# Chunk products ordered by shape, and the inverse's second form made by transposes that ScalarE copies

## The reference, cut to what matters

```python
proj = rmsnorm(x, g_mix) @ w_in            # columns: RWKV | MLA | gates
# RWKV-7, for each of 16 heads of 64, token by token:
sa = S @ kk_t
S  = S * w_t[None, :] + outer(v_t, k_t) - outer(sa, kk_t * a_t)
y_t = S @ r_t
# then group norm, bonus, gate; y_a = y @ w_o_a
# MLA: latent attention over past and new latents; y_b = o @ w_o_b
h = x + (sigmoid(Ga) * y_a + sigmoid(Gb) * y_b) @ w_out
h = h + (silu(causal_conv(gate)) * up) @ w_ffn_down   # gate, up = rmsnorm(h) @ w_ffn_in
y = rmsnorm(h, g_final)
```

## Time and profile before

| | us |
|---|---|
| median of 3 timed runs | 2621.8 (2618.93 to 2631.11) |
| profiled execution | 2617.77 |
| its span, first to last instruction | 2616.1 |
| TensorE busy | 2551.1 (98%) |
| TensorE weight loads busy | 2353.6 (90%) |
| VectorE busy | 1201.2 (46%) |
| ScalarE busy | 848.4 (32%) |
| TensorE's share of the chain that ended last | 95% |
| mean granted TensorE clock | 0.995 |

### The profile page before, as it was taken

The page is one execution under the profiler, slowest core; times in us unless marked ns, Lnnn a source line. Parts: engine busy times, 40 slices in busy tenths (PEclk is TensorE's granted clock), DMA queues, the critical chain, the costliest instruction groups (busy, mean ns, idle before and its releaser), DMA issues.

```text
span 2616.1 us, 40662 instructions
## 1 busy us (share of the span) xinstructions
PE 2551.1 (98%) x15484; PEld 2353.6 (90%) x15484; DVE 1201.2 (46%) x1855; ACT 848.4 (32%) x1247; POOL 108.4 (4%) x182
## 2 busy tenths in 40 slices
PE   6999999999999999999999899999999999999997
PEld 6888888888888999999987799999878999999886
DVE  4566566665644333334433444444333444444233
ACT  4332233322223333334422433333222333333232
POOL 3000000000001010000000000000000000000010
PEclk9999999999999999999999999999999999999999
DMA  5321222212244343334453344444333444444443
GB/s 171 90 63 43 55 68 69 67 40 60 61 104 123 104 121 101 102 90 129 127 168 121 96 128 127 123 127 128 121 121 130 127 125 124 128 128 126 143 126 129
DMA packets 414494, 283.46 MB, mean 108 GB/s; under 512 B 31729, under 2 KB 392691, under 8 KB 413409
## 3 DMA queue, kind: packets, MB, share of 16 engines
q1 hardware_dynamic: 405600, 259.16, 33.7%
q0 software_dynamic: 8832, 23.43, 3.1%
HBM read 275.62 MB, written 6.92 MB: 108 GB/s over the span
## 4 chain that ended last, share of the span: by engine, by line
PE 95%; DVE 3%; ACT 1%; issue 1%; DMA 1%; POOL 0%; DVEq 0%; SPq 0%; POOLq 0%; ACTq 0%
PE banks L1392 19%; PE banks L836 17%; PE banks L838 17%; PE banks L837 17%; PE banks L315 2%; PE banks L418 2%; PE banks L429 2%; PE banks L433 2%; PE banks L847 2%; PE banks L848 2%; PE banks L849 2%; PE banks L484 1%; PE banks L483 1%; PE banks L1255 1%; PE banks L508 1%
## 5 line engine op out<-in xcount | busy, mean ns | idle before, releaser
L826 DVE TENSOR_TENSOR w_lo<-w_raw,w_hi 128x1024 fp32r<-128x1024 f32 x482 | 590.2, 1225 | 978.2 <-ACT w_hi L821 976.5
L836 PE MATMUL banks<-x_hi,w_hi 128*128 128x384 f32 x2640 | 910.0, 345 | 7.4 <-DVE w_lo L826 7.4
L838 PE MATMUL banks<-x_hi,w_lo 128*128 128x384 f32 x2640 | 883.4, 335 | 0.0
L837 PE MATMUL banks<-x_lo,w_hi 128*128 128x384 f32 x2640 | 882.9, 334 | 0.0
L821 ACT ACTIVATE w_hi<-w_raw 128x1024 fp32r<-128x1024 f32 x482 | 511.2, 1061 | 1041.2 <-PE banks L838 605.1
L836 PEld LDWEIGHTS banks<-x_hi,w_hi 128*128 128x128 f32 x2640 | 496.0, 188 | 22.6 <-DVE w_lo L826 9.3
L837 PEld LDWEIGHTS banks<-x_lo,w_hi 128*128 128x128 f32 x2640 | 496.3, 188 | 4.8
L838 PEld LDWEIGHTS banks<-x_hi,w_lo 128*128 128x128 f32 x2640 | 495.6, 188 | 0.0
L1392 PE MATMUL banks<-w_hi,act_hi 128*128 128x512 f32 x528 | 164.0, 392 | 4.7 <-DVE h_rows L1951 2.4
L1392 PE MATMUL banks<-w_hi,act_lo 128*128 128x512 f32 x528 | 163.9, 392 | 0.0
L1392 PE MATMUL banks<-w_lo,act_hi 128*128 128x512 f32 x528 | 163.7, 391 | 0.0
(11 more groups left out here) (390 smaller groups left out, 2606.5 us busy)
## 6 DMA issues: line engine op xcount, KB each, us to landing
w_raw<-in_w_ffn_in SPq DMA_DIRECT2D x176, 512.0 KB, 4.0
w_raw<-in_w_in SPq DMA_DIRECT2D x144, 512.0 KB, 3.8
w_raw<-in_w_ffn_down SPq DMA_DIRECT2D x88, 512.0 KB, 3.6
w_raw<-in_w_out SPq DMA_DIRECT2D x32, 512.0 KB, 3.6
w_raw<-in_w_o_a SPq DMA_DIRECT2D x16, 512.0 KB, 3.9
w_raw<-in_w_o_b SPq DMA_DIRECT2D x16, 512.0 KB, 3.9
w_raw<-in_w_in SPq DMA_DIRECT2D x20, 256.0 KB, 3.7
w_ukv_head<-in_w_ukv POOLq DMA_DIRECT2D x8, 512.0 KB, 4.2
```

Of the source, the lines that this page charges most:

```text
L826: nc.vector.tensor_tensor(lo[:, s], raw[:, s], hi[:, s].bitcast(F32), ALU.subtract).then_inc(lo_done, 1)
L836: nc.tensor.matmul(out, hi[:, s, k, :], xh[:, kt, :], start=kt == 0, stop=False)
L837: nc.tensor.matmul(out, hi[:, s, k, :], xl[:, kt, :], start=False, stop=False)
L838: last = nc.tensor.matmul(out, lo[:, s, k, :], xh[:, kt, :], start=False, stop=kt == 15)
```

## The change

1. On levels 0 to 3 the product for `t_y` (line 433) and VectorE's subtraction (726) are gone. Instead, levels 1 to 4 begin with TensorE's transposes of the `t_x` that the level before has updated, and ScalarE copies them into `t_y`. Level 4 keeps its update of `t_y`.
2. Levels 0 to 3 get a second piece, behind the update product; the end of the round has four pieces instead of eight.
3. The cuts move: on ScalarE cut 2 comes between the copies of levels 2 and 3, cut 3 behind the last copy, cut 4 in the chunk steps, cut 5 ahead of the state rows; VectorE's follow.
4. In the chunk steps the outputs come first, both heads of each kind together, with both products from u and then the signal for y; then the gain's products from v, and then those from u. VectorE no longer waits for y.

The semaphores `t_x_ps` and `t_x_done` become `form_ps` and `form_done`, which count five times a round.

```diff
             for lv in range(5):
                 if lv == 0:
-                    pe.wait_ge(E("t_x_done"), f + 1)
+                    pe.wait_ge(E("form_done"), f * 5 + 1)
                 else:
-                    pe.wait_ge(E("t_done"), f * 9 + (2 * lv - 1))
+                    pe.wait_ge(E("t_done"), f * 5 + lv)
+                    for i, t in units(lv - 1):
+                        last = transpose(head_tile(2, i, t), t_x[:, 3 * i + t, :])
+                    last.then_inc(E("form_ps"), 1)
                 for i, t in units(lv):
                     u = 3 * i + t
                     last = mm_(head_tile(g_bank(lv), i, t), n_t[:, u, :], t_x[:, u, :], start=True, stop=True)
                 if lv == 0:
                     pe.wait_ge(E("mt_done"), f + 1)
                 else:
-                    pe.wait_ge(E("t_done"), f * 9 + 2 * lv)
+                    pe.wait_ge(E("form_done"), f * 5 + (lv + 1))
                 if lv < 4:
                     for i, t in units(lv):
                         u = 3 * i + t
                         last = mm_(head_tile(10 - g_bank(lv), i, t), t_y[:, u, :], t_g[:, u, :], start=True, stop=True)
-                    last.then_inc(E("dt_ps"), 1)
-                for i, t in units(lv):
-                    u = 3 * i + t
-                    last = mm_(head_tile(2, i, t), t_g[:, u, :], t_y[:, u, :], start=True, stop=True)
+                else:
+                    for i, t in units(lv):
+                        u = 3 * i + t
+                        last = mm_(head_tile(2, i, t), t_g[:, u, :], t_y[:, u, :], start=True, stop=True)
                 last.then_inc(E("dt_ps"), 1)
+                if lv < 4:
+                    pieces(1)
 
...
                 gain = [ps[heads(i), 4, 0:64] for i in range(2)]
                 yo = [ps[heads(i), 5, cols] for i in range(2)]
                 for i in range(2):
-                    mm_(gain[i], tok[r0:r0 + 64, 0, t, heads(i)], v[r0:r0 + 64, t, heads(i)], start=True, stop=False)
                     mm_(yo[i], v[:, t, heads(i)], c_k[:, 3 * i + t, cs], start=True, stop=False)
-                    if c:
+                if c:
+                    for i in range(2):
                         mm_(yo[i], st[:, 1, :], rh[:, i, cols], start=False, stop=False)
                 pe.wait_ge(E("u_done"), f * 4 + (c + 1))
-                mm_(yo[0], un[:, 0, heads(0)], c_b[:, t, cs], start=False, stop=True)
+                for i in range(2):
+                    last = mm_(yo[i], un[:, 0, heads(i)], c_b[:, 3 * i + t, cs], start=False, stop=True)
+                last.then_inc(E("y_ps"), 1)
+                for i in range(2):
+                    mm_(gain[i], tok[r0:r0 + 64, 0, t, heads(i)], v[r0:r0 + 64, t, heads(i)], start=True, stop=False)
                 for i in range(2):
                     last = mm_(gain[i], tok[r0:r0 + 64, 1, t, heads(i)], un[r0:r0 + 64, 0, heads(i)],
                                start=False, stop=True)
                 last.then_inc(E("state_ps"), 1)
-                mm_(yo[1], un[:, 0, heads(1)], c_b[:, 3 + t, cs], start=False, stop=True).then_inc(E("y_ps"), 1)
...
             pieces(4)
             if more:
                 pe_s0(f + 1)
-            pieces(8)
+            pieces(4)
...
             if more:
                 nc.scalar.preload_act_table_set("sigmoid_and_others")
             act.wait_ge(E("bonus_done"), f + 1)
-            cut(2)
+            for lv in range(1, 5):
+                n = NT if lv < 4 else 2 * P
+                act.wait_ge(E("form_ps"), f * 5 + (lv + 1))
+                fn(t_y[:, :, :].rearrange("p (h t) c -> p h (t c)", h=2)[:, :, 0:n], ps[:, 2:4, 0:n], ACT.Copy)\
+                    .then_inc(E("form_done"), 1)
+                if lv == 2:
+                    cut(2)
+            cut(3)
             if more:
                 act_gate_sigmoids(f + 1)
                 nc.scalar.preload_act_table_set("natural_log_exp_and_others")
...
-            cut(3)
             if more:
                 act_kk_square(f + 1)
+            cut(4)
+            if more:
                 act_exps_early(f + 1)
             act.wait_ge(E("yd_ps"), f + 1)
             act.wait_ge(E("y_ps"), f * 4 + 4)
             fn(yb, ps[:, 5, 0:NT], ACT.Copy).then_inc(E("y_raw_done"), 1)
-            cut(4, 0)
             act.wait_ge(E("y_centred"), f + 1)
             fn(sq_y, yc, ACT.Square).then_inc(E("y_sq_done"), 1)
-            cut(4, 1)
+            cut(5)
...
-            cut(5)
...
-                if lv == 1:
-                    cut(1)
+                if lv in (1, 3):
+                    cut(1 + lv // 2)
+                dve.wait_ge(E("dt_ps"), f * 5 + (lv + 1))
                 if lv < 4:
-                    dve.wait_ge(E("dt_ps"), f * 9 + (2 * lv + 1))
                     tt(by_head(t_x, n), by_head(t_x, n), made(10 - g_bank(lv), n), S).then_inc(E("t_done"), 1)
-                seen = 2 * lv + 2 if lv < 4 else 9
-                dve.wait_ge(E("dt_ps"), f * 9 + seen)
-                tt(by_head(t_y, n), by_head(t_y, n), made(2, n), S).then_inc(E("t_done"), 1)
-                dve.wait_ge(E("t_done"), f * 9 + seen)
+                else:
+                    tt(by_head(t_y, n), by_head(t_y, n), made(2, n), S).then_inc(E("t_done"), 1)
+                dve.wait_ge(E("t_done"), f * 5 + (lv + 1))
...
-            cut(2)
             if more:
                 dve_key(f + 1, ch)
+            cut(3)
...
-
-                    dve.wait_ge(E("y_ps"), f * 4 + (c + 1))
```

More of the change, by code:

```diff
@@ L407, in pe_rwkv @@
                 last = transpose(head_tile(2, i, t), t_y[:, 3 * i + t, :])
-            last.then_inc(E("t_x_ps"), 1)
+            last.then_inc(E("form_ps"), 1)
             pieces(1)
@@ L440, in pe_rwkv @@
                 last.then_inc(E("c_ps"), 1)
-            pe.wait_ge(E("t_done"), f * 9 + 9)
+            pe.wait_ge(E("t_done"), f * 5 + 5)
             if more:
@@ L580, in act_rwkv @@
             cut(0)
-            act.wait_ge(E("t_x_ps"), f + 1)
-            fn(t_x[:, :, :].rearrange("p (h t) c -> p h (t c)", h=2), ps[:, 2:4, 0:NT], ACT.Copy).then_inc(E("t_x_done"), 1)
+            act.wait_ge(E("form_ps"), f * 5 + 1)
+            fn(t_x[:, :, :].rearrange("p (h t) c -> p h (t c)", h=2), ps[:, 2:4, 0:NT], ACT.Copy).then_inc(E("form_done"), 1)
             cut(1)
@@ L789, in dve_rwkv @@
                 dve_k_mod(ch)
-            cut(4)
+            cut(5)
             if more:
@@ L802, in dve_rwkv @@
                 dve_alpha_beta(f + 1, ch)
-            cut(5)
+            cut(6)
             if more:
@@ L806, in dve_rwkv @@
                 dve_value(f + 1)
-            cut(6)
             cut(7)
@@ L1502, in act_cut, with cut @@
             def act_cut(f):
-                def cut(k, part=None):
+                def cut(k):
                     q, s = divmod(k, 2)
                     t = f * 4 + (T_FT + 4 + q)
-                    if s == 0 and part != 1:
+                    if s == 0:
                         if q == 0:
@@ L1512, in cut @@
                             taken_mixed(t - 1, q - 1)
-                    if part == 0:
-                        return
                     if s == 0:
@@ L1522, in _, with last_cut @@
                 act_rwkv(f, act_cut(f), ch)
-            def last_cut(k, part=None):
+            def last_cut(k):
                 q, s = divmod(k, 2)
                 t = T_MLA + q
-                if s == 0 and part != 1:
+                if s == 0:
                     if k == 0:
@@ L1531, in last_cut @@
                         taken(t - 1, t - 1, cc[:, q - 1])
-                if part != 0:
-                    act_hi(t + s, 1 - s)
+                act_hi(t + s, 1 - s)
             act_rwkv(FT - 1, last_cut, ch, more=False)
```

## The result

Five runs of the changed kernel took 2599.85 to 2606.4 us, median 2604.26; five of the kernel before took 2618.93 to 2633.27, median 2625.51. The ratio is 0.9908 (95% interval 0.988 to 0.9936): faster by 0.9%, or 21 us. So 2604.26 lies 14 us above the forecast. The profiled execution of the changed kernel took 2600.29, its span is 2598.6, 17.5 less than before, and the mean granted clock is 0.989 where it was 0.995.

What follows compares the result with a forecast made beforehand. TensorE, busy 98% of the span, was taken as the bound. Levels 2.2 + chunk steps 1.6 = 3.8 us a round, times 8 = 30, off the profiled 2617.8 gave 2588, taken as 2590; range 2580 to 2609.

Steps and rivals of the forecast that it cites:

- the forecast's own: Whole kernel: the range 2582 to 2598 us around the forecast of 2590, given a chance of 0.62.
- A: Rival, recurrence: levels gain, chunk steps don't, since VectorE paces all four; 2600, by the timed runs 2602; chance 0.16.
- B: Rival, levels: each new boundary costs 0.14 us, so they gain little; 2605, up to 2609; chance 0.14.
- The levels: Inverse's levels in the recurrence: transposes replace second products; 2.2 us a round saved, lower end 1.0.
- Levels of four units I put at the same: Inverse's levels with four units instead of six: each step saves the same 0.55 us.
- The chunk steps: Recurrence's chunk steps: products grouped by shape save 1.6 us a round, lower end 0.5, upper 2.0.
- The tail: End of a round: four pieces, 4.16 us of cover, leave; 2.3 us stay, so it costs nothing.
- C: Rival, round's tail: its cover is gone and the next round's front comes late; 2629 at 8.1 us late; chance 0.04.
- D: Rival, whole change: nothing is gained, since what is removed was hidden; 2618 to 2622; chance 0.02.
- E: Rival, levels: each transpose costs its latency, 3.9 us come back a round; 2619 to 2622; chance 0.02.
- The last line of the prediction: Wrong if a level takes over 6.4 us, the head shows idle time, or stages behind the recurrence change in length.
- no transfer is asked for sooner than in the tail of now: SP's and POOL's queues: order kept and weight halves used more evenly, so no load is needed earlier.

Runs made afterwards that it cites:

- e1: Changed kernel without its reordering of the chunk steps, which stand as in the kernel before: 2617.16 us, ratio 0.9956.
- e4: Changed kernel with the eight products of a short sequence grouped by shape, four of 128 rows, then four of 16: 2581.51 us, ratio 0.9827.
- e9: Kernel before with grouped sequence products and the new order of the chunk products, levels as before: 2599.52 us.
- e8: e4 with the transposes of levels 1 to 4 (22 a round) issued twice: 2604.17 us.
- e10: e4 with another copy of the same size ahead of each of ScalarE's four copies of the second form in a round: 2579.92 us.
- e11: e4 with the four copies of the second form made by VectorE, ahead of its mask, instead of ScalarE: 2579.82 us.
- e2: Kernel before with only the chunk steps' products reordered: 2615.9 us, ratio 0.9964.
- e5: Kernel before with only the eight products of a short sequence grouped by shape, as in e4: 2611.84 us, ratio 0.9944.
- e7: e4 with the last c_kv tile's copy and the squares of c_kv ahead of a weight split on ScalarE, behind the last round: 2577.9 us.
- e3: Changed kernel with 16 transposes more, 1.7 us, ahead of the first short sequence of the attention stage: 2603.79 us, ratio 0.9905.
- e6: e4 with the gain's first pair of products (keys and v) ahead of the wait for u in each chunk step: 2580.66 us.

## Why the prediction was right, and where it was off

- **The number, in part luck.** 2604.26 is inside the stated range, but outside the forecast's own (2582 to 2598), and where rivals A (2602) and B (2605 to 2609) stood. By the time alone one of them would have won; only the rows and the experiments tell that it was the forecast's mechanism, less a loss that no rival named. The range held because those rivals had widened it.
- **The levels, 2.2 a round.** Right in the mechanism and a little small: 2.6 by the rounds of e1, 18.0 us by e4 against e9. A level takes 5.92 where 5.89 was counted. "Levels of four units I put at the same" was too little: with the piece counted in, the two steps gained 0.62 and 0.69 us (4.88 + 1.04 to 5.30, 3.98 + 1.04 to 4.33), not 0.55. The transposes are priced by e8 (0.11), and e10 and e11 show the cover of the copy.
- **The chunk steps, 1.6 a round.** Right: 1.6 by e2, 12.3 us by e9 against e5. Rival A is out by its mechanism, though its time is 2 us from the measured one.
- **The tail.** Right: no wait at the head with four pieces less; rival C did not come. B, D and E are out by the same rows.
- **What failed** is the step from the sum to the time: "2588. The median of the timed runs stands 4.0 above it, the lowest 1.1; I take 2590". It took the profiled execution as the measure of both kernels, and every stage behind the recurrence as unchanged. The last line of the prediction named a change in those stages as what would make it wrong. That execution had the clock at 1.00 in the whole sequences' stage; the changed kernel's had six falls there, 9.4 us, and 3.4 us more went later. In the medians the edit of e4 and e5 brings 8.7 us more to the changed kernel than to the one before (22.7 against 14.0), and 30.3 less 8.7 is the 21.6 between the medians of the two: the same numbers added another way, no second proof. What speaks for the clock apart from them are the six falls in the trace and the granted clocks of the runs (0.988 against 0.992).
- **A second, smaller one:** the prediction had that "no transfer is asked for sooner than in the tail of now" and took the loads as no cost. The load ahead of the squares came later, and ScalarE's queue passed the delay on to TensorE: 2.3 us more of waiting (4.1 against 1.8); e7 takes the whole wait away, for 3.6. It is inside the 30.3, against 33 that the rounds gave (4.1 x 8). So that 30.3 meets the sum's 30 is in part luck: the levels brought more than counted, and this took it back.
- **Open:** why the low clock comes more often in the changed kernel. Up to the end of the group both traces show the same instructions at the same times (3.30 us, 19 matmuls, weight loads 2.33), and only one of them is followed by the fall. e3 says that a shift of 1.7 us doesn't decide it. What is shown is that the falls in this stage hang on this group (e4, e5), not how, nor why the stages after it lost 3.4 us.

## What to carry to other kernels

Price instructions by the start of the next one and the round by a line that runs once in it: that held to 0.3 us a round here. Then ask which stage behind the change is fragile, by the spread of the runs and their granted clocks, before the profiled execution is taken as typical. Where small products of different row counts alternate, try them grouped: here it was worth 14.0 us in the kernel before and 22.7 in the changed one, where it gave as much as the change itself.

## What the hardware showed beyond this

- Eight products of 128 and 16 rows in turn take 3.2 us, 0.4 each; by shape 2.07, 0.26 each. So six changes fewer save 1.14 us, 0.19 for each, near the 0.14 read in the earlier trace rows. The Trainium skill ("TensorEngine Tiling (Array Packing)", Key Properties) says that a change of tiling mode makes TensorE drain first. The trace agrees in that a change costs time, 0.19 us here; it doesn't show a drain as such.
- The kernel before varies by 20 us on one code (29 runs on three chips, 2617.7 to 2637.7), and the time goes with the granted clock, 0.995 for the shortest run and 0.987 for the longest. On one chip, seven runs of it span 7.4 us and four of it with the group in order (e5) 2.6. Other grouped kernels span 0.7 to 7.9 us, so much of the spread, but not all, came out of one group of eight short products, run eight times.
- Filling a wait of TensorE can be worth nothing: 4.8 us of idle time went in e6 for 0.9 us.
